# HGRN2 levels scaled in place by running products, gate features through a wide product, modulation columns by transposes, and rewritten orders of steps for three engines

## What is computed

```python
def hgrn2_recurrence(q, k, v, logf):
    b = jnp.cumsum(logf, axis=-2)
    def step(state, xs):
        decay = jnp.exp(jnp.where(incl, b_i[..., :, None, :] - b_i[..., None, :, :], -jnp.inf))
        attn = jnp.einsum("bhtd,bhsd,bhtsd->bhts", q_i, k_i, decay)
        o_i = (jnp.einsum("bhtd,bhde->bhte", q_i * jnp.exp(b_i), state)
               + jnp.einsum("bhts,bhse->bhte", attn, v_i))
...
f = lower_bound + (1.0 - lower_bound) * jax.nn.sigmoid(f_raw)
k = 1.0 - f; logf = jnp.log(f)
...
mod = jax.nn.silu(c) @ w_ada[l] + b_ada[l]        # six vectors: shift, scale, gate, twice
logits = hn @ w_in[:, the 14 gate columns]        # Fox forget, mLSTM input and forget gates
```

## Time and profile before

| | us |
|---|---|
| median of 3 runs | 1134.78 (1133.39 to 1135.26) |
| the profiled execution, its own time | 1137.42 |
| its span, first to last instruction | 1135.6 |
| PE busy | 1091.9 (96%) |
| DVE busy | 797.0 (70%) |
| ACT busy | 617.5 (54%) |

### The profile page before, as it was taken

How to read it: one execution, slowest core, us unless ns; L and a number is a source line. 1 busy time by engine, 2 the same in 40 slices (tenths; PEclk the granted TensorE clock), 3 DMA queues, 4 the chain that set the end, 5 groups by cost and what they waited for, 6 DMA issues and landing times.

```text
span 1135.6 us, 18650 instructions
## 1 busy us (share of the span) xinstructions
PE 1091.9 (96%) x7532; PEld 978.7 (86%) x7532; DVE 797.0 (70%) x1084; ACT 617.5 (54%) x695; POOL 13.0 (1%) x13
## 2 busy tenths in 40 slices
PE   6999999999988999999999999999999888999998
PEld 6999999999875799989899987669986658999986
DVE  5999974787327679789797955747886556555653
ACT  5774542653233576769668643675675445444331
POOL 0100000000000000000000000002000000000000
PEclk9999999999989999999999999998999899999999
DMA  8444332335305663434333354774444055555460
GB/s 326 161 181 145 136 127 90 131 130 185 118 32 196 234 237 112 149 113 149 117 144 113 135 199 151 293 315 156 143 147 182 20 187 194 179 180 178 167 214 19
DMA packets 26292, 181.29 MB, mean 160 GB/s; under 512 B 3040, under 2 KB 3296, under 8 KB 4960
## 3 DMA queue, kind: packets, MB, share of 16 engines
q1 hardware_dynamic: 25056, 174.66, 42.3%
q10 hardware_dynamic: 1152, 5.45, 1.3%
HBM read 179.04 MB, written 1.05 MB: 159 GB/s over the span
## 4 chain that ended last, share of the span: by engine, by line
PE 82%; DVE 7%; ACT 7%; issue 2%; DMA 1%; POOL 0%; ACTq 0%; SPq 0%; DVEq 0%; POOLq 0%
PE PS L922 80%; ACT WH L1368 2%; DVE WL L1800 2%; ACT L1735 1%; PE PS L1075 1%; DMA layer<-xt 1%; PE PS L1291 1%; DVE PS L1768 0%; DVE YL L1812 0%; DMA RAW<-wst 0%; PE PS L1153 0%; DVE layer_ln L2128 0%; POOL layer L2358 0%; DVE layer L2105 0%; ACT layer L1378 0%
## 5 line engine op out<-in xcount | busy, mean ns | idle before, releaser
L922 PE MATMUL PS<-XTH,WH 128*128 128x256 f32 x1392 | 406.9, 292 | 3.8 <-DVE XTL L2017 3.8
L922 PE MATMUL PS<-XTL,WH 128*128 128x256 f32 x1392 | 397.1, 285 | 0.0
L922 PE MATMUL PS<-XTH,WL 128*128 128x256 f32 x1392 | 396.9, 285 | 0.0
L1800 DVE TENSOR_TENSOR WL<-RAW,WH 128x2048 fp32r<-128x2048 f32 x138 | 316.7, 2295 | 113.1 <-ACT WH L1368 110.6
L1368 ACT ACTIVATE WH<-RAW 128x2048 fp32r<-128x2048 f32 x138 | 262.6, 1903 | 211.0 <-PE PS L922 207.0
L922 PEld LDWEIGHTS PS<-XTH,WH 128*128 128x128 f32 x1392 | 270.6, 194 | 7.0 <-ACT XTH L1525 4.6
L922 PEld LDWEIGHTS PS<-XTL,WH 128*128 128x128 f32 x1392 | 270.6, 194 | 2.4 <-issue 2.4
L922 PEld LDWEIGHTS PS<-XTH,WL 128*128 128x128 f32 x1392 | 270.3, 194 | 0.0
L922 PE MATMUL PS<-WH,YH 128*128 128x512 f32 x224 | 90.7, 405 | 3.7 <-DVE YL L1812 2.6
L1735 ACT ACT_TABLE_LOAD x71 | 91.1, 1283 | 1.7 <-ACT norms L1533 0.3
L922 PE MATMUL PS<-WH,YL 128*128 128x512 f32 x224 | 87.9, 393 | 0.0
(11 more groups left out here) (294 smaller groups left out, 1284.8 us busy)
## 6 DMA issues: line engine op xcount, KB each, us to landing
RAW<-wst SPq DMA_DIRECT2D x162, 1024.0 KB, 4.9
LNW<-lnrow ACTq DMA_DIRECT2D x3, 1024.0 KB, 4.8
RAW<-wst SPq DMA_DIRECT2D x4, 512.0 KB, 4.9
layer<-xt SPq DMA_DIRECT2D x2, 512.0 KB, 5.7
XR<-x ACTq DMA_DIRECT2D x1, 1024.0 KB, 5.9
out<-X SPq DMA_DIRECT2D x4, 256.0 KB, 2.1
CST<-cst ACTq DMA_DIRECT2D x1, 640.0 KB, 8.8
PT<-pt SPq DMA_DIRECT2D x1, 512.0 KB, 5.7
```

Source lines behind the costliest of these rows:

```text
L922: return pe.matmul(o, lhsT, rhs, start=start, stop=stop)
L1800: tt(WL[:, i % RAW_RING, 0:n], RAW[:, i % RAW_RING, 0:n], as_float(WH[:, k % SPLIT_RING, 0:n]), ALU.subtract).then_inc(vector_done, 1)
```

## The change

The HGRN2 levels no longer go through logarithms. FS keeps f itself (two groups' worth). `hy:g:0` multiplies q by f. `hy:g:i` (i from 1) multiplies, in place, the later half of each block of q by the running product at the earlier half's end, and the earlier half of k by the running product kept at the later half's start, and then joins the two products in FS. `hf` and `hx` are gone on ACT and DVE, and HB, HE and HX with them. `hm:g:i` multiplies HK by HQ where it multiplied HX by itself. Because q and k are scaled in place, `hy:g:i` now waits for `hm:g:i-1`.

`gates` is one feature-major product: stationary is a 128-column slice of WGW, of which 14 columns are the gates', and 256 tokens move (24 matmuls for 48); DVE copies the 14 rows, and two transposes turn them. A DVE step `wg2` prepares WGW. `adat` for the eight column-wise modulation vectors is 4 transposes for 4 fp32 matmuls by a column of ones, and DVE sums four columns with a reduce before it adds the bias. PE issues 6 matmuls of ONES by ONES, 512 columns wide, ahead of its first step. Tensors start at multiples of 64 bytes instead of 32: RAW, WH, WL, X, XTH, XTL, YH, YL and CST stay where they were; LNW, the layers' arenas, EH and EL move by 32 to 224 bytes. The three orders are new throughout.

```diff
             out.append((later(step, "hm", g, i, on="T", banks=(0, 1) if i % 2 else (2, 3), readers="V",
                               read_in=("hp", g, i)), 1.0))
+            out.append((later(step, "hy", g, i + 1, on="V"), 0.0))
...
-            if i + 2 <= NL:
-                out.append((later(step, "hx", g, i + 2, on="VS"), 0.0))
-            out.append((later(step, "hy", g, i + 1, on="V"), 0.0))
...
-        at = [(nc.sbuf_base + 31) // 32 * 32]
+        at = [(nc.sbuf_base + 63) // 64 * 64]
...
+        WGW = place("WGW", wg_at, [P, 2 * KC * NG + P], F32R)
+        GTR = CV2[:, 0, 0:T]
...
-                    last = mm(PS[:, step.banks[0], j:j + 1], MROW[:, j * P:(j + 1) * P], ONES[:, 0:1])
+                    last = pe.transpose(PS[:, step.banks[0], j * P:(j + 1) * P], MROW[:, j * P:(j + 1) * P], ident)
...
-                        x = HX[:, i % 2 * HG + h, c * P:(c + 1) * P]
-                        last = mm(PS[:, step.banks[c], h * P:(h + 1) * P], x, x)
+                        m, s = g % 2 * HG + h, slice(c * P, (c + 1) * P)
+                        last = mm(PS[:, step.banks[c], h * P:(h + 1) * P], HK[:, m, s], HQ[:, m, s])
...
-            def t_gates(step, c):
+            def t_gates(step, part):
+                if part:
+                    pe.wait_ge(vector_done, vector_at("gates", 0))
+                    for c in range(NT):
+                        last = pe.transpose(PS[:, step.banks[0], c * NG:(c + 1) * NG], GTR[0:NG, c * P:(c + 1) * P],
+                                            ident[0:NG, 0:NG])
+                    last.then_inc(tensor_done, 1)
+                    return
                 xt_ready(4)
-                s = slice(c * P, (c + 1) * P)
-                products(PS[:, step.banks[0], 0:NG],
-                                [((XTH[:, k, s], XTL[:, k, s]), (WGH[:, k, :], WGL[:, k, :])) for k in range(KC)]).then_inc(tensor_done, 1)
+                pe.wait_ge(vector_done, vector_at("wg2"))
+                wl, wh = ([WGW[:, (a * KC + k) * NG:(a * KC + k) * NG + P] for k in range(KC)] for a in range(2))
+                products(PS[:, step.banks[0], 0:T], [((wh[k], wl[k]), x_tile(k)) for k in range(KC)]).then_inc(tensor_done, 1)
...
             pe.wait_ge(gpsimd_done, gpsimd_at("setup"))
+            for _ in range(6):
+                mm(PS[:, 7, :], ONES[:], ONES[:].unsqueeze(1).to_broadcast([P, 4, P]))
...
+                parts4 = PS[:, b, :].rearrange("p (j a n) -> p j a n", j=4, a=4)[:, :, :, 0]
+                link(dve.tensor_reduce(MODT[:, r, o:o + 4], parts4, AX.X, ALU.add))
+                tt(MODT[:, r, o:o + 4], MODT[:, r, o:o + 4], v("bada", r * KC + o, 4), ALU.add).then_inc(vector_done, 1)
...
+            def v_hy(g, i):
+
+                r = slice(g % 2 * HG, (g % 2 + 1) * HG)
+                q, k, f = HQ[:, r, :], HK[:, r, :], FS[:, r, :]
+                if i == 0:
+                    dve.wait_ge(tensor_done, tensor_at("hd", g))
+                    tt(q, q, f, ALU.mult).then_inc(vector_done, 1)
+                    return
+                dve.wait_ge(tensor_done, tensor_at("hm", g, i - 1))
...
+                tt(x[:, :, s:2 * s], x[:, :, s:2 * s], y[:, :, 0:1].to_broadcast([P, n, s]), ALU.mult)
+                link(tt(z[:, :, 0:s], z[:, :, 0:s], y[:, :, s:s + 1].to_broadcast([P, n, s]), ALU.mult))
+                tt(y[:, :, 0:1], y[:, :, 0:1], y[:, :, s:s + 1], ALU.mult).then_inc(vector_done, 1)
```

More of the change, by code:

```diff
@@ L385, in plan @@
         u()
[L386 removed]
+    interleave([(lambda: None, 1.0)] + start(0), values(0))
     for g in range(HGRN_GROUPS):
@@ L410, in plan @@
     ada(4)[0]()
-    for c in range(NT):
-        unit("gates", c, on="TV")
+    step("wg2", on="V")
+    unit("gates", 0, on="TV")
+    unit("gates", 1, on="TV")
     feat(8)
@@ new lines @@
+ada:3:0 hm:3:2 first:z1:3:1 hm:3:3 z1:3:1 hm:3:4 ada:3:1 hm:3:5 adat:3 out:1:0:0 hm:3:6 out:1:1:0 hc:3 out:1:0:1 ho:3
+out:1:1:1 hr:3:1 hr:3:0 out:1:0:2 pl:1:0 out:1:1:2 first:out:1:1:3 first:out:1:0:3 out:1:0:3 out:1:1:3 xt:2:0:0 pl:1:1
+ada:8:0 ada:8:1 xt:2:0:1 xt:2:1:0 xt:2:1:1 ada:6:0 ada:6:1 adat:8 first:gate:1:0:0 first:gate:1:0:1 gate:1:0:0
+gate:1:0:1 first:gate:1:1:0 adat:6 first:gate:1:1:1 gate:1:1:0 gate:1:1:1 ada:7:0 ada:7:1 ada:9:0 ada:9:1 xt:4:0
+xt:4:3 xt:4:1 xt:4:2 ada:4:0 adat:7 adat:9 ada:4:1 gates:0 first:feat:8 gates:1 feat:8 first:feat:0 qn:1:2 feat:0
@@ new lines @@
+first:gate:1:0:1 rms:0:0:0 split:87:101 gate:1:0:1 first:gate:1:1:1 rms:0:1:0 rms:0:0:1 gate:1:1:1 rms:0:1:1 ada:7:1
+xt:4:0 xt:4:2 ada:9:1 xt:4:3 xt:4:1 split:88:108 ada:4:1 split:89:109 ga gb split:90:110 feat:8 split:91:111 qn:1:2
+feat:0 split:92:112 qn:0:0 feat:1 qn:0:1 split:93:113 feat:2 qn:0:2 split:95:115 split:94:114 feat:3 split:96:116
+feat:5 split:97:117 feat:4 feat:6 split:98:118 qn:1:0 feat:7 split:99:119 qn:1:1 score:0 split:100:120 score:1 score:2
+val:0:1 turn:0 split:101:123 turn:1 score:3 turn:2 gm score:4 pv:1 turn:3 score:5 pv:3 turn:4 turn:5 split:102:124
@@ L582 @@
-first:gate:1:0:1 split:87:101 gate:1:0:1 adat:6 first:gate:1:1:1 rmsb:0:0 gate:1:1:1 rmsb:0:1 xt:4:3 xtl:4:2 xt:4:1
-adat:7 xtl:4:0 xtl:4:1 xtl:4:3 adat:9 mod:1 gates:1 split:88:108 gates:0 ga split:89:109 gb gd gsp split:90:110 gcol
-split:91:111 qn:1:2 split:92:112 qn:0:0 split:93:113 qn:0:1 split:94:114 qn:0:2 feat:3 split:95:115 grow:0
-split:96:116 feat:4 grow:1 mb split:97:117 split:98:118 qn:1:0 gm score:0 qn:1:1 split:99:119 ratio:0 score:1
-split:100:120 score:2 ratio:1 split:101:123 ratio:2 score:3 split:102:124 score:4 ratio:3 ratio:4 pv:1 score:5
@@ new lines @@
+hp:3:2 hy:3:3 split:76:85 hy:3:4 hp:3:3 hy:3:5 hy:3:6 hp:3:5 hp:3:4 split:77:86 adat:3 split:78:87 hy:3:7 split:79:88
+hp:3:6 hz:3 split:80:89 split:81:90 hr:3:0 split:82:91 split:83:92 mod:0 hr:3:1 first:out:1:1:3 first:out:1:0:3
+lna:1:0 lnb:1:0:0 out:1:0:3 out:1:1:3 lna:1:1 lnb:1:0:1 lnb:1:1:0 lnb:1:1:1 split:84:98 xt:2:0:0 xt:2:0:1 split:85:99
+adat:8 wg2 xt:2:1:0 xt:2:1:1 split:86:100 first:gate:1:0:1 split:87:101 gate:1:0:1 adat:6 first:gate:1:1:1 rmsb:0:0
+gate:1:1:1 rmsb:0:1 xt:4:3 xt:4:1 adat:7 xtl:4:2 xtl:4:0 xtl:4:3 xtl:4:1 adat:9 split:88:108 gates:0 split:89:109
```

336 lines of the change are left out of this document (135 added, 201 removed).

## The result

The changed kernel takes **1096.09 us** (median of 4 executions, 1094.91 to 1098.11); the kernel before, run beside it, takes 1134.09 (4 executions, 1133.07 to 1135.26). The ratio is **0.9666, interval 0.9646 to 0.9687**. The profiled execution after takes 1095.09 us, its span is 1093.3 and its mean granted clock 0.997 (before: 1137.42, 1135.6 and 0.981). Of the four executions of the changed kernel two have a mean clock of 0.997 and two of 0.993; these two take 2 to 3 us longer (1097.09 and 1098.11). Three executions of the kernel before beside later runs took 1207, 1609 and 4259 us and are left out of every comparison.

A forecast was written before the change was run, and what follows sets the result against it. PE was taken as the bound, busy 1091.9 of 1135.6 us and losing time in seams. Terms summed to -27.5 us, 1109.9 against the profiled 1137.4, so 1107 against the median 1134.8; range 1098 to 1123.

The forecast's parts named there:

- Late heads: Attention heads, 875 to 917 us: pv in pairs and moved value and modulation steps save 3 us, bounds 0 and -8.
- GDN: End of GDN group 1: matmuls placed behind gks and pl:0:0 fill PE's waits, -7.5 us, bounds -3 and -10.6.
- Start: Kernel start: warm-up products speed ba and the first weight product starts earlier, -3.5 us, bounds -5 and +2.
- Tails: The two tails: lnb pieces run together, then the split, so gate products start earlier; -4 us together, bounds 0 and -7.
- adat: Eight modulation turns: four transposes replace eight fp32 matmul records each, -2 us, bounds 0 and -2.4.
- Gates: Gate features: 24 wide products replace 48 narrow ones taking 9.5 us; -7 us, bounds -4 and -9.
- HGRN2: HGRN2 levels: savings on DVE and ACT hidden, in-place waits cost 0.5 us a group; +2 us, bounds 0 and +10.
- Rival 2: HGRN2's in-place chain: hy ends over 1 us late at each of 28 levels, kernel slower, 1147; chance 0.07.
- MLP seam: Ahead of the MLP: the last rms step and rmsb:1:1 no longer stand behind ACT's split; -2.5 us, bounds 0 and -4.
- places in memory: Tensor starts at 64 bytes, whole kernel: no effect, 0 us, bounds -1 and +1.
- signs of being right: First product at high pace before 16 us; PE near 95% busy after gks; gates within 5.5 us; HGRN2 above 99%.
- Rivals 1, 3 and 4: Whole kernel: seams give way to next waits, 1120 (0.20); low clock oftener, 1121 (0.08); nothing measurable, 1134 (0.05).

The follow-up runs named there:

- pairs_apart: Changed kernel with a step of another kind put between neighbouring heads' paired score or pv steps in TensorE's order; 1099.95 us, ratio 0.9701.
- heads_old: Changed kernel with the old orders for the attention heads, from score:0 to pv:15, on three engines; 1105.91 us, ratio 0.9742.
- heads_new: Kernel before with the changed kernel's orders for the attention heads alone, on three engines; 1124.39 us, ratio 0.9906.
- no_warm: Changed kernel without the six products of ones ahead of ba; 1097.72 us, ratio 0.9669.
- home32: Changed kernel with the named tensors placed at multiples of 32 bytes instead of 64; 1094.99 us, ratio 0.9645.
- gdn_end_old: Changed kernel with the old orders in GDN group 1, while setup, wg and c1 keep a late place on DVE; 1112.46 us, ratio 0.9798.
- hgrn_old: Changed kernel with the HGRN2 block in its old code and orders (logarithms, exponentials, scaled copies); 1094.95 us, ratio 0.9645.
- adat_old: Changed kernel with the modulation rows turned by products with ones as before, without the sum on DVE; 1098.96 us, ratio 0.9690.
- gates_old: Changed kernel with the gate products in their old form and order, without wg2; 1101.21 us, ratio 0.9699.
- seam_old: Changed kernel with the old orders between pv:15 and ff:0 on three engines; 1098.88 us, ratio 0.9683.
- pair_14_15: Changed kernel with score:14 moved right behind score:15, ahead of adat:5, as one more pair; 1100.26 us, ratio 0.9694.

## Why the prediction was right or wrong

**Late heads, -3: the step that failed.** I took the stretch's loss from idle time and clock ("PE idles 5.3 us and loses 3.4 to a clock of 0.92"), 8.7 in all, and a third of it as gain. Idle time gave 3.0 and the clock 3.3, already twice that. The other 6.5 us come from what I counted as full work: a busy PE with half its rows or columns. pairs_apart puts 5.1 of them on the overlap; the last 1.4 no run takes apart, but by the ends of the steps 0.8 of them lie in four value products (`val:0:1` to `first:val:1:1`: 11.80 us in heads_old, 11.00 in the changed kernel). I read "runs `pv` in pairs" in the order and did not ask what a pair costs. A row of the kernel before had it (866.44: 8 passes in 0.93 us where 4 take 0.92), and the Trainium skill's Part 3, cited above, states it; I did not weigh it. With 5.8 us for the pairs the heads' term would have been -3 - 5.8 = -8.8, the sum -33.3 and the forecast 1101.5; most of what is left to 1096.1 is GDN.

**GDN, -7.5.** Group 1 gave 9.1, inside its bounds (-3 to -10.6). The two moved parts stood 25 and 24 steps earlier in TensorE's order, not 40. All of the 10.6 us of loss but the two waits for ACT (0.84 + 1.33, the "about 2" of the forecast) came back; the deduction for new small waits in the doubling levels was wrong, they didn't come. Group 0 gave 3.5 that I had not priced: about 1.4 are a low stretch of the profiled execution of before (heads_new, with the same orders there, takes 177.1 us instead of 178.5). The other 2 are most likely the new orders of group 0: the stretch stays at 174.9 to 175.1 without the warm-up (no_warm), with the old places (home32) and with the old orders of group 1 (gdn_end_old), but no run takes back group 0's orders alone.

**Start, -3.5.** Measured -1.9. `ba` began 0.2 us late (forecast 0.4) and took 4.3 us (forecast 3.5); the step "starts near 13.4" held with 13.9; "runs 24 matmuls at 0.12" failed, since the clock fell during `ba` and stayed low until 18.6 us. In home32 and hgrn_old, where this low stretch is half as long, `k:0:1` ends a further 0.9 to 1.0 us earlier.

**Tails -4, adat -2.** Together 4.7 instead of 6. adat_old makes adat worth 2.9 to 3.4 us, beyond its lower bound of -2.4; without the low stretch in the second tail's seam, which varies between executions, it is about 1.8, close to the 2 that I took. What is left for the order of `lnb`, by subtraction from the 4.7, is 1.3 to 2.9; no run takes that order back.

**Gates, -7.** Measured -7.5, and gates_old gives 6.5 to the new form. What I expected to come again, a low stretch after the sparse seam, didn't come in the profiled execution. At the high level the old form would take 48 x 0.112 = 5.4 us against 3.2, so most of what the term gained is low clock that went: its size was right, partly by luck. 27 narrow products stand 0.11 us apart at the high level in gates_old. The table that I took from the Trainium skill ("TensorE: Matmul & The Clock Gate", Back-to-back issue gap) would have made the edit a loss of 1.4 us; those rows decide against it here. The section itself gives that table for a product by itself and says that it counts too little at small widths, where each product loads weights, and I had left that out.

**HGRN2, +2.** Measured +0.5. The waits of the in-place chain are there (PE idles 2.5 us in 224, 98.9% busy, a little under the "above 99%" that I named), but other waits went: from `gate:0:1:1` to `out:1:1:3` it idles 3.3 us, and 3.0 in hgrn_old, which takes 317.4 us there against 317.7. Rival 2 needed over 1 us at each of 28 levels and got about 0.1. DVE's 38 us and ACT's 61 us less (of 224) bought nothing, as the earlier trace rows said.

**MLP seam, -2.5, and places in memory, 0.** Measured -3.4 (seam_old 4.4 with a low stretch) and 0.

Of my signs of being right, PE in the stretch behind `gks` is busy 91% (26.71 of 29.30 us) at clock 1.00, not 95%.

Rivals 1, 3 and 4 did not come; rival 3 came the other way round, in the profiled execution: all low stretches but the first are gone. They made 41 us of the span of before, at most 20 us lost in all (half their length, less what fell into idle time), and part of several terms above is theirs. I had priced them seam by seam and discounted most; in this execution they went all at once.

## What to carry to other kernels

Where products have 64 rows or 64 columns of weights, look in the timeline for two of them side by side before you take a busy TensorE as bound: two halves in turn take the time of one, so neighbouring heads belong next to each other, if the second is ready by then. Price a seam at its idle time plus half of the low stretch that follows, as far as TensorE is busy in it, and expect both to go together when the seam is filled. And when one order of steps is put among steps of another, its cost can be a mismatch of its own: compare the stretch with both parents before you read the total.

## What the runs showed that I had not expected

- Two halves of the array overlap fully in fp32 at two passes a product: 0.108 us a pass instead of 0.216 with 256 columns moving, 0.055 instead of 0.109 with 128.
- The number of low stretches varies between executions of one kernel. In 17 executions of the kernel before, the mean clock is 0.987 to 0.980 and the time 1132.7 to 1139.6 us, in clusters near 1133, 1135.5 and 1137.4; a difference of 2 us between two profiles can be one such stretch.
- The clock can fall while TensorE is called busy in every instant: in gates_old it does so during products with 14 columns moving (busy 3.00 in 3.00 us), behind a sparse seam (5.15 of 7.70 us busy ahead of them). Which of the two it answers to, no run shows.
- A short wait can cost its own length twice: in pair_14_15 2.32 us of waiting were followed by `adat:5` at 2.08 us instead of 1.1, in a low stretch, and `score:0` to `pv:15` was 4.6 us longer.
